# Presums moved beside the attention, mix jobs interleaved with the Fourier transform, and new orders at five other places

## What is computed

```python
# first block: windowed attention, then a squared-relu MLP
h = x + swa_mixer(rms_norm(x, attn_norm), w_qkv, sinks, w_o)        # 16 heads, window 128, ALiBi
a = relu(rms_norm(h, mlp_norm) @ w_up); x = rms_norm(h + (a * a) @ w_down, final_norm)
# second block, even layer, for x and for ctx, with modulation from c and c_ctx
a_val, a_glu, a_gate, b_val, b_gate = split(pre(x) @ e_w_in)
u = silu(layernorm(dwconv(a_val * sigmoid(a_glu)) + conv_b))
y_a = (u @ pw_w + pw_b) * silu(a_gate)
f = fftn(b_val by groups of 128, axes=(time, channel), norm='ortho').real
y_b = einsum('blgd,gde->blge', f, fw) * silu(b_gate)
x = x + gate * (concat(y_a, y_b) @ e_w_out)
# second block, odd layer: short convolution beside window attention with rope, then the last norm
x = x + gate * (concat(y_c, y_d) @ o_w_out); return rms_norm(x, final_norm_2)
```

## Time and profile before

| | |
|---|---|
| median of 3 runs | 2080.65 us (2079.83 to 2083.32) |
| the profiled execution's own time | 2084.15 us |
| its span | 2082.4 us |
| TensorE busy | 1990.7 us, 96% |
| VectorE busy | 1472.5 us, 71% |
| ScalarE busy | 899.0 us, 43% |
| GpSimd busy | 331.2 us, 16% |
| TensorE's granted clock, mean | 0.982 of full |

### The profile page before, as it was taken

The page is one execution under the profiler, slowest core; times in us unless marked ns, Lnnn a source line. Parts: engine busy times, 40 slices in busy tenths (PEclk is TensorE's granted clock), DMA queues, the critical chain, the costliest instruction groups (busy, mean ns, idle before and its releaser), DMA issues. The chain is left out here.

```text
span 2082.4 us, 26661 instructions
## 1 busy us (share of the span) xinstructions
PE 1990.7 (96%) x9870; PEld 1632.8 (78%) x9870; DVE 1472.5 (71%) x2523; ACT 899.0 (43%) x1725; POOL 331.2 (16%) x282
## 2 busy tenths in 40 slices
PE   6999999999998999999999999999989999999997
PEld 4877787877887788877788888788877877888785
DVE  7277877678887988878789995864363356777634
ACT  4265644645455444323531242732252235555522
POOL 2033323343431000000400010000020012222200
PEclk9999999999999999999999999999999999999998
DMA  3266401587775454443131175133122211101312
GB/s 130 70 165 200 102 21 41 200 262 250 233 245 178 154 163 149 166 146 120 51 132 40 32 180 153 46 126 132 41 97 80 71 47 38 39 26 41 117 41 91
DMA packets 76064, 240.31 MB, mean 115 GB/s; under 512 B 8992, under 2 KB 20896, under 8 KB 72480
## 3 DMA queue, kind: packets, MB, share of 16 engines
q1 hardware_dynamic: 69216, 191.07, 27.1%
q0 software_dynamic: 4272, 38.75, 8.0%
q10 hardware_dynamic: 2448, 8.79, 1.1%
HBM read 194.58 MB, written 68.16 MB: 126 GB/s over the span
## 5 line engine op out<-in xcount | busy, mean ns | idle before, releaser
L177 PE MATMUL banks<-u2H,wH 128*128 128x512 f32 (+1 forms) x704 | 261.0, 371 | 5.0 <-POOL u2L L439 3.0
L178 PE MATMUL banks<-u2L,wH 128*128 128x512 f32 (+1 forms) x704 | 256.9, 365 | 0.0
L179 PE MATMUL banks<-u2H,wL 128*128 128x512 f32 (+1 forms) x704 | 256.8, 365 | 0.0
L172 DVE TENSOR_TENSOR wL<-raw,wH 128x1024 fp32r<-128x1024 f32 x101 | 125.5, 1244 | 73.0 <-ACT wH L167 72.8
L1117 POOL TENSOR_SCALAR logits<-logits,stat 128x256 f32<-128x256 f32 (+3 forms) x96 | 121.3, 1276 | 334.4 <-DVE stat L992 334.4
L2451 DVE SCALAR_TENSOR_TENSOR conv_out<-conv_in,par,conv_out 128x1295 f32<-128x1295 f32 x108 | 162.6, 1564 | 0.6
L177 PEld LDWEIGHTS banks<-u2H,wH 128*128 128x128 f32 x704 | 133.8, 190 | 28.5 <-issue 5.7
L179 PEld LDWEIGHTS banks<-u2H,wL 128*128 128x128 f32 x704 | 133.5, 190 | 21.5
L178 PEld LDWEIGHTS banks<-u2L,wH 128*128 128x128 f32 x704 | 133.8, 190 | 20.2 <-issue 0.2
L167 ACT CAST wH<-raw 128x1024 fp32r<-128x1024 f32 x101 | 105.6, 1047 | 81.0 <-DMA raw<-in_wstream 78.9
L177 PE MATMUL banks<-kpH,formH 128*128 128x512 f32 x336 | 132.6, 395 | 5.6 <-DVE hm L2107 3.3
(11 more groups left out here) (415 smaller groups left out, 5190.6 us busy)
## 6 DMA issues: line engine op xcount, KB each, us to landing
raw<-in_wstream SPq DMA_DIRECT2D x101, 512.0 KB, 3.5
mod_w<-in_mod_w SPq DMA_DIRECT2D x48, 512.0 KB, 5.4
hidden_scratch<-hid SPq DMA_DIRECT2D x64, 256.0 KB, 5.5
sraw<-in_sstream SPq DMA_DIRECT2D x28, 512.0 KB, 6.2
sums_scratch<-in_sblocks POOLq DMA_DIRECT2D x12, 1024.0 KB, 9.6
kpR<-hidden_scratch SPq DMA_DIRECT2D x24, 512.0 KB, 5.3
formR<-sums_scratch SPq DMA_DIRECT2D x28, 256.0 KB, 2.7
side_sum<-side_tap POOLq DMA_DIRECT2D x11, 647.5 KB, 5.8
```

Source lines behind the costliest of these rows:

```text
L172: eng.tensor_tensor(wL[:, u % R, :], raw[:, u % R, :], wH[:, u % R, :].bitcast(F32), ALU.subtract)\
L177: first = pe.matmul(out, aH, bH, start=start, stop=False, skip_group_check=more)
L178: pe.matmul(out, aH, bL, start=False, stop=False, skip_group_check=more)
L179: return first, pe.matmul(out, aL, bH, start=False, stop=stop, skip_group_check=more)
```

## The change

No product, split or vector operation is added or taken away; what changes is order, waits, banks and the size of the gate loads. (1) All 24 presum steps stand beside the attention, both lanes together after 12 of its 16 steps. (2) `kp_load(0)` is issued at an earlier product. (3) `pe_cols` at the head of the MLP, and that of the context in `ein`, come later. (4) In the four-step stage, splits of `dft`+3 to +5 move forward; mix jobs of both kinds alternate by a table, two of them before the third part of the transform; waits are per chunk rather than for everything; gates come in 24 pieces. (5) At the end of `eout` the residual and squares of job 22 move forward; at the head of `oin` the norm's short matmuls come later, the jobs run as two pairs, and `oin`+2 is loaded and split earlier. (6) At the tail, the residual of the last job stands before the last two scalings of the first tile. The core of it (of `MIX` and `SP_KP` a line):

```diff
-        PRESUMS = [[(2 * pair + lane, part) for part in range(PRESUM_STEPS) for lane in range(2)] for pair in range(2)]
+        PRESUMS = [[(2 * pair + lane, part) for lane in range(2)] for pair in range(2) for part in range(PRESUM_STEPS)]
+        BESIDE = [k for k in range(16) if k not in (6, 7, 14, 15)]
 
         def presums_beside(pool, k):
-            if k < len(PRESUMS[0]):
-                presum_step(pool, *PRESUMS[0][k])
+            if k in BESIDE:
+                for group, part in PRESUMS[BESIDE.index(k)]:
+                    presum_step(pool, group, part)
...
-        SP_KP = {(PAIRS - 1, 0): [0], (PAIRS - 1, 2): [1], (PAIRS - 1, 6): [2], (PAIRS, 0): [3], (PAIRS, 3): [4], (PAIRS + 3, 6): [5, 6],
+        SP_KP = {(PAIRS - 2, 6): [0], (PAIRS - 1, 2): [1], (PAIRS - 1, 6): [2], (PAIRS, 0): [3], (PAIRS, 3): [4], (PAIRS + 3, 6): [5, 6],
...
             for n in range(PAIRS):
                 form_sums(pool, n)
-                if 0 < n <= len(PRESUMS[1]):
-                    presum_step(pool, *PRESUMS[1][n - 1])
...
-                if (j, k) == (0, 3):
+                if (j, k) == (0, 4):
                     norm2.pe_cols(pe, 1, 16)
...
-                if (j, k) == (2, 2):
+                if (j, k) == (3, 0):
                     norm4_cols_ctx(pe)
...
+        MIX = [("pw", 0, 0), ("pw", 0, 1), ("pw", 0, 2), ("fw", 0, 0), ("pw", 1, 0), ("fw", 0, 1), ("pw", 1, 1), ("fw", 0, 2),
...
+        MIX_BANKS = (2, 0, 1, 6, 7, 3)
+        MIX_AHEAD = 2
...
+                sp.dma_start(gt[j % 8][:, 0:n], gates_d[mix_chunk(j)][:, c0:c0 + n]).then_inc(gt_loaded[j % 8][0], 16)
...
+                    pe.wait_ge(f_lo, (13 if ti == 2 else 9) + c)
...
+                    pe.wait_ge(s_lo, HALF * ti + HALF)
                 slot = begin(u)
-                if oc == 4 and ti == 0:
-                    pe.wait_ge(s_lo, len(jobs))
                 if j < 6:
-                    pe.wait_ge(f_lo, 16)
+                    pe.wait_ge(f_lo, (3, 4, 10, 1, 2, 12)[j])
                 else:
                     pe.wait_ge(mix_v, j - 5)
...
+            transform(0)
+            transform(1)
+            for j in range(MIX_AHEAD):
+                mix(j)
+            transform(2)
+            for j in range(MIX_AHEAD, len(MIX)):
+                mix(j)
...
-            split_lo(dve, W0["dft"] + 3)
+                if ti == 1:
+                    split_lo(dve, W0["dft"] + 3)
...
-            split_lo(dve, W0["dft"] + 4)
-            split_lo(dve, W0["dft"] + 5)
...
+                if j == 3:
+                    split_lo(dve, W0["dft"] + 4)
+                if j == 9:
+                    split_lo(dve, W0["dft"] + 5)
...
+            for j in range(MIX_AHEAD, len(MIX)):
+                y_low(j - MIX_AHEAD)
+                gated_value(j)
...
+            eout_square(act, 22)
             norm5.act_high(act, 5)
-            eout_square(act, 22)
...
+            eout_residual(dve, 22)
             split_lo(dve, W0["oin"] + 1)
-            eout_residual(dve, 22)
+            eout_add(dve, 22)
             norm5.dve_value(dve, 6)
-            eout_add(dve, 22)
...
-            pe.wait_ge(mix_v, len(mjobs))
-            pe.wait_ge(y_lo, len(mjobs))
-
             def between(pe, j, k):
+                if j < T3 + 1:
+                    v, ti = EOUT[j]
+                    pe.wait_ge(y_lo, mix_at(k, ti) + 1)
...
+            load_unit(sp, O0 + 2)
             norm5.wait_ready(sp, 3 * KC)
             sp.dma_start(rope[:], t["rope"]).then_inc(S["rope_loaded"], 16)
-            for u in range(O0 + 2, O0 + 12):
+            for u in range(O0 + 3, O0 + 12):
                 load_unit(sp, u)
...
-                if (j, k) in ((0, 2), (0, 3)):
-                    norm5.pe_cols(pe, k - 1, 24)
-                if (j, k) in ((0, 5), (0, 6)):
-                    norm5.pe_spread(pe, k - 4)
+                if (j, k) == (0, 5):
+                    norm5.pe_cols(pe, 1, 23)
+                if (j, k) == (1, 6):
+                    norm5.pe_spread(pe, 1)
+                if (j, k) == (2, 2):
+                    norm5.pe_cols(pe, 2, 24)
+                if (j, k) == (2, 6):
+                    norm5.pe_spread(pe, 2)
 
             run_jobs(pe, O0, OIN_KV, TILES2, hl2(w2H, w2L), lambda j: OIN_KV[j][0] * T3 + OIN_KV[j][1], S["kv_done"], S["k_drained"],
-                     norm5, 2, between, need=lambda j: 0, trail=2)
+                     norm5, 2, between, need=lambda j: 0, trail=2, groups=[(0, 1), (2, 3)])
...
+                if j == 2 * KC:
+                    split_lo(dve, O0 + 2)
...
-            oout_scale(dve, 0)
+            add(14)
+            oout_scale(dve, 0, range(0, KC - 2))
             residual(15)
+            oout_scale(dve, 0, range(KC - 2, KC))
+            add(15)
```

More of the change, by code:

```diff
@@ L45 @@
 EPS = 1e-6
-STAGES = [("qkv", 10), ("wo", 8), ("mlp", 12), ("ein", 20), ("dft", 6), ("fw", 1), ("pw", 2),
+STAGES = [("qkv", 10), ("wo", 8), ("mlp", 12), ("ein", 20), ("dft", 6), ("pw", 1), ("fw", 1), ("pw2", 1),
           ("eout", 8), ("oin", 26), ("oout", 8)]
@@ L517, in run_jobs @@
         def run_jobs(pe, base, jobs, tiles, rhs, bank_of, done, drained, norm=None, paired=0, between=None, ready=None,
-                     head=0, need=None, trail=0):
+                     head=0, need=None, trail=0, groups=None):
             last = {v: j for j, (v, ti) in enumerate(jobs)}
             frees = [0] + [last[v] + 1 for v in sorted(last)[:-1]]
-            steps = [(j, k - trail * j) for k in range(KC + trail * (paired - 1) if paired else 0) for j in range(paired)
-                     if 0 <= k - trail * j < KC]
-            steps += [(j, k) for j in range(paired, len(jobs)) for k in range(KC)]
+            groups = groups or ([range(paired)] if paired else [])
+            steps = [(j, k - trail * i) for group in groups for k in range(KC + trail * (len(group) - 1))
+                     for i, j in enumerate(group) if 0 <= k - trail * i < KC]
+            steps += [(j, k) for j in range(sum(map(len, groups)), len(jobs)) for k in range(KC)]
             opened = set()
@@ L2526, in four_sp @@
             sp.wait_ge(conv_step, HALF * TAPS - SIDE + 1)
-            for i, g in enumerate(order):
-                if i == 2:
-                    for u in range(W0["dft"] + 2, W0["pw"] + 2):
-                        load_unit(sp, u)
-                if i == 6:
-                    load_unit(sp, W0["eout"])
-                if i == 7:
-                    load_unit(sp, W0["eout"] + 1)
-                if i >= 2:
-                    sp.wait_ge(mix_v, 3 * (i - 1))
-                sp.dma_start(gt[:, i % 2, :], gates_d[g]).then_inc(gate_loaded[i % 2], 16)
+            for j in range(5):
+                load_gate(j)
+            load_unit(sp, W0["dft"] + 2)
+            load_unit(sp, W0["dft"] + 3)
+            sp.wait_ge(ln_sq_used, len(jobs))
+            for j in range(5, 8):
+                load_gate(j)
+            load_unit(sp, W0["dft"] + 4)
+            load_unit(sp, W0["dft"] + 5)
+            load_unit(sp, PW0)
+            load_unit(sp, FW)
+            sp.wait_ge(dft_done, 4 + 12)
+            load_unit(sp, PW1)
+            for j in range(8, len(MIX)):
+                load_gate(j)
+                if j == 17:
+                    sp.wait_ge(mix_done, mix_at(1, 2) + 1)
+                    load_unit(sp, W0["eout"])
+            sp.wait_ge(mix_done, mix_at(HALF + 3, 2) + 1)
+            load_unit(sp, W0["eout"] + 1)
         def four_pe(pe):
@@ L2589, in four_pe, with transform @@
                         m.then_inc(dft_done, 1)
-            for half in range(3):
+            def transform(half):
                 u = D0 + 4 + min(half, 1)
@@ L2951, in oin_act @@
                 act.copy(v2T[:, c0:c0 + n], bank(3 + ti, n)).then_inc(S["k_drained"], 1)
-            for y in range(2):
-                split_hi(act, O0 + 2 + y)
+            split_hi(act, O0 + 3)
             for ti in range(2):
@@ L2978, in oin_dve @@
         def oin_dve(dve):
[L2979 to L2981 removed]
+            norm5.dve_root(dve, 1)
             for j in range(KC, 3 * KC):
@@ L3229, in residual, with add @@
                     .then_inc(oout_drained, 1)
+            def add(j):
                 oout_squares.dve(dve, j, j % 2, OOUT[j][1], TN)
@@ L3233, in oout_dve @@
                 residual(j)
+                add(j)
                 if oout_split(j):
```

147 lines of the change are left out of this document (96 added, 51 removed).

## The result

The changed kernel takes 2045.11 us in the median of 4 runs (2043.79 to 2046.04), the kernel before 2081.99 (2079.83 to 2084.36) beside it: a ratio of 0.9822, 95% interval 0.9805 to 0.9839. The profiled execution's span fell from 2082.4 to 2044.2 us, and TensorE's mean granted clock rose from 0.982 to 0.990.

A forecast was written before the change was run, and what follows sets the result against it. The prediction took TensorE's idle time and its time at the lower clock as what the change could act on; terms summed to -35.9 us, 2048.2 against the profiled 2084.15, 2045 as a median, forecast range 2036 to 2051.

The forecast's parts named there:

- Presums out of the MLP: In the MLP, without presums the loads have the DMA engines to themselves and TensorE waits less: -5.4 us.
- the two larger waits for hidden values: In the MLP, 3.7 of TensorE's 4.4 us of such waits would go, with one clock loss of 1.7.
- `kp` 0: Before its cast: an earlier load ends TensorE's 3.6 us evacuation wait and 1.65 of clock loss, -5.3 us.
- Head of the MLP: There, later `pe_cols` cuts the 1.6 us wait for squares by 1.4, plus half of 1.8 clock loss: -2.3.
- Four-step stage: Transform and mix: earlier splits, `pw` jobs ahead and waits per chunk remove 8.6 us of gaps and 4.9 of clock loss: -13.5.
- The 2.0 us for `fL`: Four-step stage: two `pw` jobs before the last transform part would remove this wait for its low halves.
- The rival that alternating short jobs over six banks would keep the clock low: Transform and mix: short waits remain, so 4.9 us of clock loss stay though gaps go: 2050; chance 0.1.
- the clock loss of 4.9: Four-step stage, 1345 to 1415: time lost at TensorE's lower clock, added to 8.6 us of gaps.
- My rule, a clock loss with each stall: Whole kernel: a TensorE stall of 2 us or more is followed by about 1.7 us of lower-clock loss.
- Head of `oin`: With the end of `eout`: gaps 9.7 and clock 5.0 go, less 2.2 of new stalls and 1.7 of clock: -10.8.
- Attention: Presums there: GpSimd costs nothing, but part six meets the `hm` load and delays it by 2.5 at most: +2 us.
- the rival of a blocked GpSimd: Attention: a long presum part delays GpSimd's divisions and TensorE's transposes, 2088 us at 50 us each; chance of slower 0.04.

The follow-up runs named there:

- e1: Changed kernel with only the presums as before, 12 steps one lane at a time beside the attention and 12 in the MLP; ratio 0.9846 to the kernel before.
- e2: Changed kernel with the `kp` 0 load, the context's column sums in `ein` and the tail's order as before; ratio 0.9854 to the kernel before.
- e8: Changed kernel with the two `pw` jobs moved behind the third part of the transform, on all three engines; ratio 0.9836 to the kernel before.
- e3: Changed kernel with the whole four-step stage (splits, mix order, banks, gate pieces, waits) as before; ratio 0.9905 to the kernel before.
- e11: Changed kernel with only the load and splits of unit `oin`+2 where they stood before; 2052.81 us, ratio 0.9879 to the kernel before.
- e4: Changed kernel with the end of `eout` and the heads of `oin` and the MLP as before; ratio 0.9882 to the kernel before.
- e12: Changed kernel with only the norm's column sums, roots and spreads at the head of `oin` placed as before; 2042.94 us, ratio 0.9832 to the kernel before.
- e5: Changed kernel with the first pair's last presum part moved behind the load of `hm`, the second pair's parts one step later; ratio 0.9804 to the kernel before.
- e9: Changed kernel with the first pair's last presum part again behind the load of `hm`, run beside the unedited one; 2039.49 us, ratio 0.9816 to the kernel before.
- e10: The changed kernel run again without an edit, for comparison on the same chip; 2040.27 us, ratio 0.9819 to the kernel before.

## Why the prediction was right

The sum, -35.9 us, met -36.9 in the medians and -38.2 between the two profiled spans, and the predicted 2045 met 2045.1. That is closer than its terms, and in part luck: by the first pair of profiles they are off by -2.2 (presums), +1.4 (`oin`), -1.0 (tail), -0.7 (four-step stage), +0.6 (head of the MLP), and by +1.8 in the attention's mean, and cancel; and the 2045 was counted from a kernel before of 2080.65, which took 2081.99 beside the changed one.

**Presums out of the MLP** (-5.4, measured -7.6): the mechanism is shown by e1. The step that was too small is "the two larger waits for hidden values": all six went, 4.4 us, and the clock loss with them. What I had as the bound, 6, was passed.

**`kp` 0** (-5.3, measured -4.3 to -5.5): as predicted, SyncE issues it at once after the last modulation sum and the cast waits for nothing. e2 shows it independent of the presums.

**Head of the MLP** (-2.3, measured -1.7): the wait for the squares is gone and the clock stayed whole (1.00 in 340 to 360, 0.91 before). The division was another: the prediction gave 1.4 to the wait and 0.9 to the clock, but 1.1 us of new waits for `mL` came in place of the wait of 1.6, so most of the gain goes with the clock.

**`ein`** (0, measured +0.5 here): right within the spread there, by e2.

**Four-step stage** (-13.5, measured -14.2): the total is right and the stage is now full: 55.64 us of matmul in 56, at full clock. That VectorE could carry it was the open question, and it did with 46.1 us busy of 56. Two terms of my sum were wrong inside. The 2.0 us for `fL` were put down to the jobs ahead of the third part; e8 shows 0.7 for these. The rival that alternating short jobs over six banks would keep the clock low falls: it was 1.00. And the clock loss of 4.9 was added to the gaps as if both were independent; e3 shows the same stage time at 3.5 us less clock loss and 2.1 more wait. My rule, a clock loss with each stall, counted something that was partly hidden; what made up for it among the 7 us that the three experiments leave is open.

**Head of `oin`** (-10.8, measured -9.4, and -8.6 against the mean): the total is near, its make-up was not. The gaps shrank by 6.1 us (9.7 to 3.6; predicted 7.5) and the clock loss by 5.0 (predicted 3.3), 11.1 together for 9.4 us of time. And I added two waits, 5.6 for the squares and 3.5 for `oin`+2. Both went, but they are not two gains that can be had apart. The rope tables and the load behind them leave when the norm is done: the load at 1536.49 in e11, 47.7 us after matmul 7052 (1488.79), and at 1560.64 before, 47.5 after the same matmul (1513.17), though TensorE waited 5.6 us for the squares in the one and not in the other. A TensorE that no longer waits for the squares only comes to the unit earlier and waits there longer, 6.7 us. So with the load and its splits as before, all the rest of this place (the norm's order, the jobs in two pairs, the end of `eout`) is worth nothing: 72.3 us in e4 without it, 72.8 in e11 with it. With the load early the norm's order is worth 2.2 (e12). The early load and splits are worth 8.9 us (e11); e4 against e12, which differ in the pairs and the end of `eout` too, gives 6.2. The load did most of it.

**Tail** (-0.6, measured -1.6, of it 0.7 in the wait): the order did what was predicted, the size was too small, since only the wait was counted. VectorE's rows at the tail, the last squares right behind the two scalings.

```profile
2028.40 0.75 DVE L3318 SCALAR_TENSOR_TENSOR xo<-banks,modv,xo 128x512 f32<-128x512 f32 x1
2029.07 1.28 DVE L3302 TENSOR_TENSOR xo<-xo,norm_rs 128x512 f32<-128x512 f32 x2
2030.27 0.69 DVE L239 TENSOR_TENSOR oout_squares_acc<-oout_squares_acc,oout_squares_sq 128x512 f32<-128x512 f32 x1
```

**Attention** (+2, measured +3.8): the mechanism, the last part of the first pair meeting the load of `hm`, is shown by e5 and e9: moved away, `hm` lands after 12.3 and 13.4 us against 16.4 to 19.6 in ten profiles with it and 15.4 and 15.8 with the old presums. The landing was put off by 2.7 us in the mean of the ten (18.3 against 15.6), near the "2.5 at most"; the step that was missing is the clock: over 192 to 206 us it is 0.77, and 0.88 before, 1.5 us more of loss, and no term stood for it here as it did with the other stalls. That the rival of a blocked GpSimd did not come about is right, but by less than I wrote: the slack at the third division was 2.3 us, in e4 and e10 nothing.

## What to carry to other kernels

Two waits in a row on one engine are not a sum when the second ends at a time fixed by something else: take away the later one's cause first, or the earlier one's gain turns into a longer wait (nothing gained alone here, 2.2 with the other). A stretch of lower clock behind a stall may cost little where the engine waits again soon; check it with two executions of the same code. And a transfer moved out of one crowded place should be laid against the next large load: one part moved behind that load took 5 us off the landing of `hm` and 7 us off the stretch in the profiles, though by time it gained 3 to 4 us in one job and nothing clear in another.

## What the runs showed of the hardware

GpSimd stood 9.84 us between the two transfers of its second lane's part two (128.00 and 138.64 in the changed kernel), with no wait that the profile shows ("issue"). The traces tell what ended it. The two accumulating transfers of the first lane, issued at 124.09 and 124.67, landed at 133.34 and 138.39, and the held one left 0.25 us after the second of them. In all twelve profiles with both lanes' steps together the issue is held so, for 8.6 to 10.7 us, and ends 0.25 or 0.26 us after that landing; with one lane at a time (before and e1) none is held. The program has no wait between the two. How many transfers may be in flight was not tried.

Profiles of one execution each differ by some us in a place, at the same code: `hm` lands between 16.4 and 19.6 us after its issue in ten profiles, and the second attention (matmuls 7650 to 8400) takes 133.3 to 136.4 us, at a granted clock of 1.00 and 0.97. Other stretches agree within 0.1 us in all profiles of one order (81.5 us in the four-step stage, 204.0 in the MLP). So terms under 2 us need several profiles in the one kind of place, and one in the other.
